# Eight heads of a gated delta rule, prepared half a head apart instead of in pairs

## The reference, cut to what matters

```python
kc, vc, bc = chunks(k), chunks(v), chunks_s(beta)     # 8 heads, 8 chunks of 64
gc = jnp.cumsum(chunks_s(g), axis=-1)
decay = jnp.exp(jnp.where(tri, gc[..., :, None] - gc[..., None, :], -jnp.inf))
a_mat = jnp.where(strict, einsum(k_beta, kc) * decay, 0.0)
rhs = jnp.concatenate([v_beta, k_beta * jnp.exp(gc)[..., None]], axis=-1)
sol = lax.linalg.triangular_solve(eye + a_mat, rhs, lower=True, unit_diagonal=True)
u, w = sol[..., :dv], sol[..., dv:]
...   # then a scan over the chunks with q, k, u, w and the decays
```

## Time and profile before

| | |
|---|---|
| median of 3 runs | 2572.59 us (2569.84 to 2576.09) |
| the profiled execution, its own time | 2570.07 us |
| its span | 2568.3 us |
| TensorE (PE) busy | 2358.6 us, 92% |
| VectorE (DVE) busy | 1083.0 us, 42% |
| ScalarE (ACT) busy | 927.7 us, 36% |
| GpSimd (POOL) busy | 700.4 us, 27% |
| mean clock granted to TensorE | 0.956 of 2.4 GHz |
| chain that ended last | TensorE 75%, VectorE 11%, ScalarE 8% |

### The profile page before, as it was taken

One profiled execution on the slowest core, in us unless ns is written; L12 is line 12 of the kernel. 1 busy time (PEld: TensorE's weight loads), 2 busy tenths in 40 slices (PEclk: granted clock), 3 DMA queues, 4 the chain that ended last, 5 costly groups with the idle time before them and its releaser, 6 DMA issues.

```text
span 2568.3 us, 27012 instructions
## 1 busy us (share of the span) xinstructions
PE 2358.6 (92%) x10928; PEld 1890.4 (74%) x10928; DVE 1083.0 (42%) x1579; ACT 927.7 (36%) x1352; POOL 700.4 (27%) x417
## 2 busy tenths in 40 slices
PE   8798989997789899899999887999999999999996
PEld 4577877993467677688888676787777777888875
DVE  2476655444433432433321499513444243322333
ACT  2534424114433432533322332334552433322334
POOL 1141144001101125322223232321232353432332
PEclk9898989998899899999999898999999999999998
DMA  8222223221122123333333421232211322333341
GB/s 261 74 66 74 68 57 99 66 78 37 37 52 62 52 84 109 102 100 98 94 98 97 123 79 57 88 98 82 82 58 58 115 82 82 107 90 99 99 123 50
DMA packets 347984, 220.67 MB, mean 86 GB/s; under 512 B 18393, under 2 KB 327244, under 8 KB 347860
## 3 DMA queue, kind: packets, MB, share of 16 engines
q1 hardware_dynamic: 338462, 202.31, 27.2%
q10 hardware_dynamic: 9398, 16.62, 2.0%
HBM read 210.49 MB, written 8.41 MB: 85 GB/s over the span
## 4 chain that ended last, share of the span: by engine, by line
PE 75%; DVE 11%; ACT 8%; POOL 3%; issue 3%; DMA 1%; ACTq 0%; SPq 0%; DVEq 0%; POOLq 0%
PE ps L342 74%; DVE arena L368 4%; ACT arena L357 4%; DVE arena L360 2%; DVE scr L368 1%; PE ps L345 1%; ACT scr L357 1%; POOL wlo L360 1%; ACT whi L357 1%; ACT L353 1%; POOL arena L360 1%; DVE arena L365 1%; DVE scr L360 1%; DVE wlo L360 1%; DMA wraw<-in_w_in_dram 1%
## 5 line engine op out<-in xcount | busy, mean ns | idle before, releaser
L342 PE MATMUL ps<-hhi,whi 128*128 128x512 f32 x1664 | 679.1, 408 | 53.2 <-POOL wlo L360 30.3
L360 POOL TENSOR_TENSOR wlo<-wraw,whi 128x1024 fp32r<-128x1024 f32 (+1 forms) x164 | 391.2, 2385 | 1188.7 <-ACT whi L357 1188.7
L342 PE MATMUL ps<-hlo,whi 128*128 128x512 f32 x1664 | 662.8, 398 | 0.0
L342 PE MATMUL ps<-hhi,wlo 128*128 128x512 f32 x1664 | 661.7, 398 | 0.0
L357 ACT ACTIVATE whi<-wraw 128x1024 fp32r<-128x1024 f32 (+1 forms) x328 | 340.8, 1040 | 372.7 <-PE ps L342 304.2
L342 PEld LDWEIGHTS ps<-hhi,whi 128*128 128x128 f32 x1664 | 322.7, 194 | 133.7 <-issue 47.9
L342 PE MATMUL ps<-arena 128*128 128x128 f32 (+4 forms) x2304 | 335.4, 300 | 41.1 <-ACT arena L357 17.5
L342 PEld LDWEIGHTS ps<-hlo,whi 128*128 128x128 f32 x1664 | 322.3, 194 | 68.4 <-issue 3.7
L342 PEld LDWEIGHTS ps<-hhi,wlo 128*128 128x128 f32 x1664 | 321.1, 193 | 69.9
L360 DVE TENSOR_TENSOR wlo<-wraw,whi 128x1024 fp32r<-128x1024 f32 x164 | 213.0, 1299 | 353.0 <-ACT whi L357 352.9
L342 PEld LDWEIGHTS ps<-arena 128*128 128x128 f32 x2304 | 289.1, 197 | 72.5 <-issue 21.8
(11 more groups left out here) (190 smaller groups left out, 2678.2 us busy)
## 6 DMA issues: line engine op xcount, KB each, us to landing
wraw<-in_w_in_dram SPq DMA_DIRECT2D x99, 512.0 KB, 3.9
wraw<-in_w_ff_dram SPq DMA_DIRECT2D x64, 512.0 KB, 4.0
wraw<-in_ffn_w_up_dram SPq DMA_DIRECT2D x44, 512.0 KB, 3.9
wraw<-in_w_ada_dram SPq DMA_DIRECT2D x32, 512.0 KB, 3.9
wraw<-in_w_gate_dram SPq DMA_DIRECT2D x32, 512.0 KB, 3.9
arena<-in_w_ada_dram SPq DMA_DIRECT2D x8, 1024.0 KB, 11.7
wraw<-in_ffn_w_down_dram SPq DMA_DIRECT2D x16, 512.0 KB, 3.8
wraw<-in_w_branch_dram SPq DMA_DIRECT2D x16, 512.0 KB, 3.3
```

Source lines behind the costliest of these rows:

```text
L342: return pe.e.matmul(o, l, r, start=start, stop=stop)
L360: return q.e.tensor_tensor(o, a, b, op)
```

## The change

The heads' generators are started one by one instead of in pairs: a head starts when its v is ready, when fewer than two heads are under way and when at least ten turns have passed since the last start. Each turn then advances the live heads by one step, the older first. The loops in which a head waited for its v are taken out of `prep` of all four engines, since the new generator tests it. In the class Plan, which only notes the order of the weight blocks, the new generator is empty.

```diff
-            def prep_pairs(self):
-                for h in range(0, 8, 2):
-                    yield from both(self.prep(h, 0), self.prep(h + 1, 1))
+            def prep_heads(self):
+
+                live, h, since = [], 0, 10
+                while h < 8 or live:
+                    if h < 8 and 16 + h in self.have and len(live) < 2 and since >= 10:
+                        live.append(self.prep(h, h % 2))
+                        h, since = h + 1, 0
+                    since += 1
+                    for g in list(live):
+                        try:
+                            next(g)
+                        except StopIteration:
+                            live.remove(g)
+                    yield
...
-            weave(chain(first, paced(f.small_proj(), more)), f.prep_pairs(), 30, 100)
+            weave(chain(first, paced(f.small_proj(), more)), f.prep_heads(), 30, 100)
...
+            prep_heads = steps(0)
...
-                while 16 + h not in self.have:
-                    yield
```

## The result

The kernel with the heads half a head apart took **2587.18 us** (median of 4 runs, 2585.62 to 2588.59) against 2571.22 us for the kernel before in 4 runs of the same comparison: a ratio of **1.0068**, interval [1.0054, 1.0083]. It is slower by 16.0 us by the medians. 2581 had been predicted.

What follows compares the result with a forecast made beforehand. TensorE was taken as the bound, busy nine tenths of nearly every slice. Gaps 48.6 plus clock 5.6 made 54.2 us against 45.4 lost now: +8.8 on 2572.6 gives 2581 us; own range 2578 to 2590, whole range 2557 to 2597.

Steps and rivals of the forecast that it cites:

- The 0.9 us put on an uncovered copy: In the levels: TensorE idles 0.9 us after a T product while ScalarE copies it, if the other head has no filler.
- the 2.1 us "open": Behind a main step: VectorE's subtraction comes 3.97 us late, one head covers 1.86, leaving 2.1 us less the other's filler.
- the 2.5 for VectorE's normalising products: Heads 2/3: head 3's two normalising products, waiting for Ln and Exp, stand ahead of head 2's subtraction, a 2.5 us gap.
- Period by period: Head preparation split into stretches of one head's first half beside the former's second; estimated gaps sum to 48.6 us.
- the 2.7 us for the gates of head 4: Heads 3/4: gates hold VectorE past the main step, with modulation, a weight and taps still behind them, a 2.7 us gap.
- Four more round trips: ScalarE's Exp split from SiLU in more places, 1.3 us per switch; TensorE sees only those behind a main step.
- the clock: Half clock behind seven gaps of 1.9 us and more: 0 to 11.2 us lost, half taken, 5.6.
- The four dips: Four half-clock windows in the old head preparation, 14.9 us lost; expected to go, with short ones in their place.
- Rival 1: Regimes fill each other: half the middle gaps filled, full clock, -15.4 us, about 2557; chance 0.28.
- Rival 2: A draw: the gaps as listed and no fall of the clock, +3.2 us, about 2576; chance 0.26.
- Rival 3: Much slower: all seven gaps cost clock (+11.2), head 7 alone at 1.2 GHz (+10); +24.4, about 2597; chance 0.10.
- Rival 4: The change does not do what it says: only that the distance averages 10.5 turns; no size or chance given.

Runs made afterwards that it cites:

- before_notaps: Kernel before, with VectorE's three convolution taps on q, k and v cut to one instruction over 8 columns: 2560.01 us, ratio 0.9973.
- after_notaps: Changed kernel with VectorE's three convolution taps cut to one instruction over 8 columns: 2567.85 us, ratio 0.9995 to the kernel before.
- dist15: Changed kernel with heads starting at a distance of 15 turns (16 in fact) in place of ten: 2651.44 us, ratio 1.0328 to the kernel before.
- early_a: Kernel before, with each pair's six main steps ahead of turns 0, 3, 4, 6, 7 and 12 instead of every 3.33 turns: 2571.76 us, ratio 1.0007.
- dist1: Changed kernel with heads starting one turn apart in place of ten: 2581.04 us, ratio 1.0047 to the kernel before.

## Why the prediction was right, and where it was not

**Right: the direction and the mechanism.** The cover of the levels is lost. The 0.9 us put on an uncovered copy is 0.69 of gap and the 0.2 by which the group after it is longer. The idle time and the growth of the third line, put down to the breaks, come to 42.9 + 5.0 = 47.9 us, where 48.6 were summed. Behind a main step the 2.1 us "open" of the forecast stand as 2.03 at 253.55, 285.74 and 358.24, and the 2.5 for VectorE's normalising products ahead of a subtraction as 2.40:

```profile
270.16 0.69 DVE L360 TENSOR_TENSOR arena<-arena 128x512 f32<-128x512 f32 x1 [1.38 <-ACT arena L357]
...
271.49 0.69 DVE L360 TENSOR_TENSOR arena<-arena 128x512 f32<-128x512 f32 x1 [0.64 <-ACT arena L357]
272.10 1.28 DVE L360 TENSOR_TENSOR arena<-arena,ps 128x512 f32<-128x512 f32 x2
...
272.93 2.92 PE L342 MATMUL ps<-arena 128*128 128x128 f32 x24 [2.40 <-ACT arena L357]
```

**Period by period** (sum of gaps, predicted and measured, us): head 0 alone 6.9 and 7.1; heads 0/1 5.5 and 5.7; 1/2 5.1 and 5.9; 2/3 8.4 and 7.7; 3/4 6.55 and 3.9; 4/5 5.15 and 3.7; 5/6 3.8 and 1.8; 6/7 2.6 and 3.9; head 7 alone 4.6 and 3.1. Up to head 3 the walk through the queues holds. In 3/4 the 2.7 us for the gates of head 4 was 0.78. Each predicted 0.9 holds the 0.2 of a break, which the measured gaps don't (their sum is 42.9, and the breaks are the 5.0 above). So that the sum comes out close is in part luck: errors of both signs, up to 2.7 us in a period.

**Four more round trips** between SiLU and Exp: 11 loads became 19, as counted. What they cost was undersized in the words "of which only the ones behind a main step are seen by TensorE": without them the change would cost 5.6 to 8.0 us instead of 16.0 to 17.5. As to the Trainium skill (ScalarE: Activation LUTs, What ACT_TABLE_LOAD costs), whose 2.66 us per switch would have made two gaps 3.3 us: they were 1.88 (193.25) and 2.40 (238.50, shown above), with a switch of 1.28 us in each. The trace does not agree with the page: the longer of the two lies 0.5 us over the forecast by the row, and 0.9 us under the one by the page.

**The term that failed** is the clock. "Bounds: none of my seven gaps of 1.9 us and more costs anything, or all cost 1.6 (11.2); I take half, 5.6." It measured 13.6 us, more than the upper bound. The forecast was 48.6 + 5.6 - 45.4 = 8.8; the stretch measured 47.9 + 13.6 - (30.5 + 16.0) = 15.0. Of the 6.2 us between them the new clock term is +8.0; the gaps take 0.7 back, and the old clock, 16.0 where 14.9 was read from four windows, another 1.1. The four dips did not go, they moved.

The number of falls was about right, their price was not. The forecast priced a fall at 1.6 us, from the sample of the earlier trace rows, and took half of seven, 3.5 falls. There were four, of 4.4, 3.0, 3.1 and 3.4 us. That the number fits is in part luck too: of nine gaps of 1.88 us and more behind the first wait, three brought a fall, and the fourth fall stands behind a gap of 1.23. The sample was a short one:

```profile
685.25:688.67 3.42, 3.39 (x8) 2.74 (x9) 1.83 (x2) 1.54 (x2) 0.00 (x0) 0.50 0.58 153
```

Half clock lasts 3.42 us there and 6.8 to 10.2 us in the changed kernel's stretch. The forecast had better samples at hand: its four windows of the earlier trace rows cost 14.9 us, 3.7 each, and 3.5 falls at that price would have been 13.0. The first fall of the changed kernel (TensorE alone):

```profile
144.70 0.92 PE L345 MATMUL ps<-cst,arena 128*128 128x128 f32 x4 [2.27 <-DVE arena L360]
146.39 2.07 PE L342 MATMUL ps<-arena 128*128 128x128 f32 x8 [0.78 <-POOL arena L360]
149.15 3.78 PE L342 MATMUL ps<-arena 128*128 128x128 f32 x16 [0.69 <-ACT arena L357]
```

8 records take 2.07 and 16 take 3.78 us. The clock fell at 144.90, 0.2 us after TensorE had come back from the gap of 2.27 us and before the two small ones, and stayed at 1.2 GHz until 155.14. Why it stays down for longer in one place than in another is not shown: behind 176.44 TensorE ran without a gap, and half clock lasted until 182.44 all the same.

**The rivals.** Rival 1 (the regimes fill each other, 2557) needed idle under 35 us; it is 42.9. The rule of the Trainium skill (Perfetto Trace Analysis, Optimization Strategy) that interleaving regimes may help is not borne out here. Rival 2 (no fall of the clock, 2576) fails by the same term as the forecast. Rival 3 had one half right: its clock in the middle (11.2) is nearest to the measured 13.6. Its other half is refuted by head 7 alone, at 1.00 in the windows above with 2.46 of 15.3 us idle, where "some 17 us with a fourth idle" had been written. Rival 4 decides nothing: head after head starts 10 or 11 turns apart, as counted.

**What stays open:** what makes the clock fall behind one gap and not behind another; what half clock alone costs this stretch, since the run with filled gaps didn't isolate it; and how taps and table loads share the loss when both are gone.

## What to carry to other kernels

Before two like chains are shifted against each other to mix their regimes, ask which of their regimes is covered only by its own like: here the levels run nearly gapless beside another head's levels, and a shift of two turns keeps that while one of ten exposes each copy. With in-order queues, the price of a step placed behind a large one is everything that the large step releases on ScalarE and VectorE (here scale, table load, SiLU, three taps: 2 to 2.6 us), so cost it in the queue's order and not by its own length. Price a fall of the clock by what the falls in the same stretch cost (3.7 us each here), not by a sample from elsewhere (1.6).

## What the hardware showed that was not expected

**The length of a gap does not decide the clock.** TensorE fell to 1.2 GHz at 144.90, just behind a gap of 2.27 us; at 175.62, within one of 2.58; at 254.12, 0.6 us behind one of 2.03; and at 332.63, 1.3 us behind one of 1.23 with short work of other shapes. The gaps of 2.40 (238.50 and 272.93), 1.88 and 1.89 us, and two more of 2.03, left it at 1.00. So did the longest, 3.33 us ahead of the sums of squares at 126.06; but the same wait of 3.33 us was followed by half clock in four other runs (before_notaps, after_notaps, dist15 and early_a, there from 126.51 to 129.92). Here are two gaps of 2.03 us and the groups behind them, the first falling to half clock on its way, and the window around the gap of 2.40 at 272.93:

```profile
253.55 1.53 PE L342 MATMUL ps<-arena 128*128 128x128 f32 x8 [2.03 <-DVE arena L360]
358.24 1.13 PE L342 MATMUL ps<-arena 128*128 128x128 f32 x8 [2.03 <-DVE arena L360]
...
264.00:273.00 9.00, 6.60 (x38) 4.97 (x36) 4.45 (x7) 6.18 (x9) 1.27 (x1) 1.00 0.27 82
```

The Trainium skill (TensorE: Matmul & The Clock Gate, Why this matters for your kernels) asks for no idle gap over about 3 us between bursts of matmuls. The trace of the changed kernel does not agree, either way: the one gap over 3 us in the stretch left the clock at 1.00, and the clock fell four times where no gap reached 3 us.

**VectorE stopped by GpSimd.** The 40 instructions of the modulation in the changed kernel (min, median, max ns):

```profile
L368 DVE SCALAR_TENSOR_TENSOR scr<-wraw,mod,scr x40: 739/744/2931, 120.6 to 438.6; 128x512 f32<-128x512 f32 x40
```

One takes 744 ns in the median, and up to 2931 where GpSimd splits a weight block beside it. In dist1 above, the pair of them takes 3.50 us from 323.06, with GpSimd busy from 323.44 to 326.01: the first, begun ahead of GpSimd's, takes 744 ns, and the second takes 2833 and ends at 326.56. The mean of 1121 in the earlier trace rows is a mean over such unlike ones, so the "2 x 1.12 us" of the forecast was too much at most places and too little at the blocked ones. The Trainium skill (SBUF — State Buffer, Who interferes with whom) says that a VectorE instruction with two SBUF inputs contends with a GpSimd instruction that reads SBUF, and that the port pair they share is locked by one of them at a time. The trace agrees: the slow instruction ends 0.55 us after GpSimd's.
